# Turning the row picks of a mixture-of-experts loop round: one-hot columns stand, split rows move

## The chip, the cores and the metric

The kernel runs on one core of one Trainium2 chip. The metric is the device time in microseconds (us) of one execution; before the change the median of three runs is 2247.96 us.

## What is computed

A two-layer transformer block on 256 latent tokens and 256 context tokens of width 1024, all in float32. Each layer has three parallel token mixers (two attentions and a pooling), an output projection, and then a mixture of experts. Context tokens leave the second layer after their keys and values, so the experts see 512 tokens in layer 0 and 256 in layer 1. The part that the change touches:

```python
def hierarchical_moe(h, w_rg, b_rg, w_re, b_re, w_gate, w_up, w_down):
    lg = jnp.dot(h, w_rg, ...) + b_rg                 # 4 groups, the best one is taken
    ...
    top_p, top_i = lax.top_k(jax.nn.softmax(le_g, axis=-1), TOP_K)   # 2 of its 8 experts
    ...
    return expert_dispatch(h, experts, weights, w_gate, w_up, w_down)

def run_block(args):                                  # one of 32 experts, D 1024, hidden 512
    xb, e = args
    return (jax.nn.silu(xb @ w_gate[e]) * (xb @ w_up[e])) @ w_down[e]
```

Every token goes to two experts; an expert holds the rows that fall to it, in the order of the tokens. The results come back weighted and are added to the stream.

## The kernel before

Each engine has its own instruction stream, written out by hand, and engines wait for each other at semaphores. A layer's mixer part comes first (its matrix products use fp32r, a one-pass form, on weights and activations split into a high and a low part, lines 459 to 461). Then the norm, the router and the routing follow, then the loop over the experts, and at last a gather of the saved rows.

**Routing.** VectorE works out in a long chain of small operations (L1339 to L1376) which tokens go to which expert and in which slot; `place1` holds for each token and expert the slot number plus one, or zero. Beside it TensorE turns the normed activations back to rows (L678) and ScalarE copies them into `hr` (L999), tokens on the partitions.

**The loop** (L732 on TensorE, 16 turns of two experts, slots s = 0 and 1 of the weight buffers). An expert's rows are picked by a product with a one-hot matrix: VectorE compares `place1` with slot numbers 1 to 64 (`set_pick`, L1380) and gets for each tile of 128 tokens a matrix of 128 x 64; TensorE multiplies, in float32, with the rows standing and the 64 one-hot columns moving (`pick_x`, L702), 8 chunks of 128 features by 4 token tiles (2 in layer 1). The result is already transposed, features on the partitions, 64 slots wide, and is copied by VectorE (L1437) to `xg`. Then `gate_up` (L711) multiplies the standing 64 slots with the moving weights of gate and up, in two column halves of the array at once. ScalarE applies silu (L1032), VectorE multiplies (L1417), TensorE transposes the hidden rows (`turn_h`, L717), VectorE copies them (L1435), and `down` (L723) multiplies with the down weights. ScalarE copies the result (L1055) and saves it with DMAs on its own queue (L1012): 32 rows, and 32 more if the expert holds over 32.

The order on TensorE for one expert is: gate-up of e, first half of the pick for e + 1, turn of e's hidden rows, second half of the pick, down of e. So each half of a pick stands where TensorE would otherwise wait for silu and for the copy.

**Overflow.** An expert with more than 64 rows is done in further blocks of 64 (an `If` around a `Fori` over all possible blocks, on TensorE, VectorE and ScalarE alike), between gate-up and the turn: pick, copy, gate-up, silu, multiply, turn, copy, down, save.

**Weights.** SyncE's queue loads them, 4 MB for gate and up in four DMAs (L392) and 2 MB for down in two (L396), two experts ahead: the gate-up weights of e + 2 are issued once the hidden rows of e are turned, its down weights once e's down is done, in this order on one queue.

Of the kernel before, what the change touches and what calls it, by code (L numbers as in the profile page):

```python
# [18 lines left out]
F32 = mybir.dt.float32  # L19
F32R = mybir.dt.float32r  # L20
# [3 lines left out]
ALU = mybir.AluOpType  # L24
ACT = mybir.ActivationFunctionType
AX = mybir.AxisListType.X

P = 128
# [25 lines left out]
HALF = BLK // 2  # L54
LATENT, CONTEXT = slice(0, SEQ), slice(SEQ, NTOK)
# [75 lines left out]
def hybrid_block(nc, t, out, counts=None):  # L131
# [4 lines left out]
    with ctx:  # L136
# [48 lines left out]
        def part(base, kib, size, *dims, dt=F32):  # L185
# [18 lines left out]
        xg = [part(arena, 24 + 2 * i, 2, KC, BLK) for i in range(3)]  # L204
        pick = [part(arena, 30 + i, 1, 4, BLK) for i in range(3)]
        hid = [part(arena, 34 + i, 1) for i in range(3)]
        hid_t = [part(arena, 37 + i, 1, 2, P) for i in range(3)]
# [4 lines left out]
        r = part(arena, 16, 8)  # L212
        place1 = part(arena, 33, 1)[:, 0:4 * (NE + 2)].rearrange("p (t e) -> p t e", t=4)
# [39 lines left out]
            hrow_copied r_exp r_onehot r_pos r_exp_done routed pick_set picko_set dest_set xt_done xt_copied  # L253
            gu_done silu_done hid_done0 hid_done1 hidt_done hidt_copied down_done0 down_done1 y_copied0
            y_copied1 xto_done xto_copied guo_done siluo_done hido_done hidto_done hidto_copied downo_done
# [182 lines left out]
        def _(pe):  # L438
# [89 lines left out]
            for l in range(DEPTH):  # L528
# [144 lines left out]
                for tile in range(nt):  # L673
                    for half in range(2):
                        bank = 2 + (2 * tile + half) % 4
                        claim(bank)
                        for c in range(4):
                            mm = pe.transpose(ps[:, bank, c * P:(c + 1) * P], ht[:, 4 * half + c, tile * P:(tile + 1) * P], ident[:, :])  # L678
                        mm.then_inc(g["hturn_done"].sem, g["hturn_done"].tick(l, tile, half))
                        free[bank] = (g["hrow_copied"], (l, tile, half))  # L680
# [10 lines left out]
                nb = w_all // BLK  # L691
# [4 lines left out]
                pe.wait_ge(g["hrow_copied"].sem, g["hrow_copied"].at(l, nt - 1, 1))  # L696

                def pick_x(dst_bank, picks, sem, chunks=range(KC)):

                    for c in chunks:  # L700
                        for tile in range(nt):
                            mm = pe.matmul(ps[:, dst_bank, c * BLK:(c + 1) * BLK], hr[:, tile, c * P:(c + 1) * P], picks[:, tile, :],  # L702
                                           start=(tile == 0), stop=(tile == nt - 1))
                    if chunks[-1] == KC - 1:
                        mm.then_inc(sem, 1)

                def gate_up(bank, xs, w, sem):

                    for k in range(KC):
                        for j in range(2):  # L710
                            mm = pe.matmul(ps[BLK * j:BLK * j + BLK, bank, :].rearrange("p (g n) -> p g n", g=2), xs[:, k, :],  # L711
                                           w[:, k, 512 * j:512 * j + 512].rearrange("p (g n) -> p g n", g=2), start=(k == 0), stop=(k == KC - 1))
                    mm.then_inc(sem, 1)

                def turn_h(bank, src, sem):
                    for c in range(2):
                        mm = pe.transpose(ps[:, bank, c * P:(c + 1) * P], src[:, c * P:(c + 1) * P], ident[:, :])  # L717
                    mm.then_inc(sem, 1)
# [7 lines left out]

                if l == 0:
                    n_more = pe.alloc_register("pe_more")
                    pe.reg_mov(n_more, 0)
                pe.wait_ge(g["pick_set"].sem, (NE + 2) * l + 1)  # L730
                pick_x(0, pick[0], g["xt_done"].sem)
                with pe.Fori(0, NE // 2) as i:  # L732
                    for s in range(2):
                        e, done = 2 * i + s, NE * l + 2 * i + s
                        mine = 16 * l + i
                        pe.wait_ge(g["xt_copied"].sem, done + l + 1)
# [8 lines left out]
                        with pe.If(n > BLK):  # L745
                            with pe.Fori(1, nb) as b:
                                with pe.If(n > b * BLK):
                                    more = pe.snap(n_more, min_val=0, max_val=64)
                                    pe.wait_ge(g["picko_set"].sem, more + 1)
                                    pick_x(7, pick[2], g["xto_done"].sem)  # L750
                                    pe.wait_ge(g["xto_copied"].sem, more + 1)
                                    pe.wait_ge(g["yo_copied"].sem, more + 1)
                                    gate_up(6, xg[2], wgu[s], g["guo_done"].sem)
                                    pe.wait_ge(g["hido_done"].sem, more + 1)
                                    turn_h(7, hid[2], g["hidto_done"].sem)
                                    pe.wait_ge(g["hidto_copied"].sem, more + 1)
                                    down(6, hid_t[2], wd[s], g["downo_done"].sem)
# [47 lines left out]
        def _(act):  # L805
# [68 lines left out]
            for l in range(DEPTH):  # L874
# [121 lines left out]
                for tile in range(nt):  # L996
                    for half in range(2):
                        act.wait_ge(g["hturn_done"].sem, g["hturn_done"].at(l, tile, half))
                        nc.scalar.activation(hr[:, tile, 512 * half:512 * half + 512], ps[:, 2 + (2 * tile + half) % 4, :], ACT.Copy) \  # L999
                            .then_inc(g["hrow_copied"].sem, g["hrow_copied"].tick(l, tile, half))  # L1000
# [6 lines left out]
                nb = w_all // BLK  # L1007

                def save_rows(src, row, signal, first=0, rows=BLK):
                    for j in range(2):  # L1010
                        at = BLK * j + first
                        act.dma_start(y_rows[bass.ds(row, rows), j * 512:(j + 1) * 512], src[at:at + rows, :]) \  # L1012
                            .then_inc(signal.sem, 16)

                if l == 0:
# [6 lines left out]
                    act.sem_inc(g["yo_saved"].sem, 32)  # L1022
# [3 lines left out]
                with act.Fori(0, NE // 2) as i:  # L1026
                    for s in range(2):
# [11 lines left out]
                        with act.If(n > BLK):  # L1039
                            with act.Fori(1, nb) as b:  # L1040
                                with act.If(n > b * BLK):
                                    more = act.snap(n_more, min_val=0, max_val=64)
                                    act.wait_ge(g["guo_done"].sem, more + 1)
                                    nc.scalar.activation(act_g[2], ps[:, 6, 0:256], ACT.Silu).then_inc(g["siluo_done"].sem, 1)
                                    act.wait_ge(g["downo_done"].sem, more + 1)
                                    act.wait_ge(g["yo_saved"].sem, more * 32 + 32)
                                    nc.scalar.activation(ysb[2], ps[:, 6, :], ACT.Copy).then_inc(g["yo_copied"].sem, 1)
                                    act.wait_ge(g["yo_copied"].sem, more + 2)
                                    save_rows(ysb[2], act.snap(row + b * BLK, min_val=0, max_val=2 * NTOK), g["yo_saved"])
# [594 lines left out]
```

## Time and profile before

| | |
|---|---|
| median of 3 runs | 2247.96 us (2247.88 to 2249.99) |
| profiled execution | 2246.29 us, its span in the profile 2244.5 us |
| granted TensorE clock, mean | 0.961 |
| TensorE busy | 2070.9 us, 92% of the span |
| VectorE, ScalarE, GpSimd busy | 647.1, 513.0, 156.2 us |
| read from memory | 537.15 MB |
| expert loop of layer 0, first gate-up to last down | 662.15 to 1285.04 us |
| expert loop of layer 1 | 1690.37 to 2206.21 us |

The slices of the page divide the span into 40 parts of 56.1 us. A float32 matmul stands in the profile as two records, as does its weight load; an fp32r matmul as one. Mean durations of pipelined matmuls overlap, so what one costs in a stream is its group's busy time divided by its count, or the distance in the chain.

### The profile page before, as it was taken

The numbers are of one execution on the slowest core, as the hardware profiler recorded it, in microseconds if no ns is written. First come the engines' busy times: TensorE is split into PE (matmuls) and PEld (weight loads), VectorE is DVE, ScalarE is ACT, GpSimd is POOL, SyncE is SP. The second block draws the span as 40 slices with busy tenths as digits, with TensorE's granted clock in tenths as the row PEclk, the third lists the DMA queues.
The fourth block names the chain that finished last, engine by engine and source line by source line (L and its number), as shares of the span: only waits on it lengthen the run. The fifth ranks groups of instructions, "written<-read, shape, count | busy, mean of one in ns | idle before, by whom it ended". The sixth has DMA issues, their size and how long they took to land.

```text
span 2244.5 us, 31445 instructions
## 1 busy us (share of the span) xinstructions
PE 2070.9 (92%) x11703; PEld 1323.6 (59%) x11704; DVE 647.1 (29%) x1392; ACT 513.0 (23%) x1028; POOL 156.2 (7%) x190
## 2 busy tenths in 40 slices
PE   5899999999979999999999959988979999999995
PEld 2666665678746655556555548766965444454443
DVE  1565354345441010110101056455451101110112
ACT  2444333432230001000000044444130001111111
POOL 0053030000000000000000013231000000000000
PEclk9899999999979999999999979989999999999997
DMA  6445554223158898857688523232457879999993
GB/s 233 167 150 190 204 204 154 102 75 99 47 225 345 357 366 364 366 220 303 265 366 361 224 92 123 75 92 93 151 215 310 335 309 421 421 421 421 421 420 113
DMA packets 95915, 551.01 MB, mean 245 GB/s; under 512 B 14034, under 2 KB 15010, under 8 KB 42596
## 3 DMA queue, kind: packets, MB, share of 16 engines
q1 hardware_dynamic: 83108, 526.89, 59.5%
q0 software_dynamic: 4224, 11.35, 1.8%
q10 hardware_dynamic: 8512, 11.81, 1.5%
q8 instruction: 47, 0.77, 0.1%
q14 instruction: 24, 0.20, 0.0%
HBM read 537.15 MB, written 12.85 MB: 245 GB/s over the span
## 4 chain that ended last, share of the span: by engine, by line
PE 78%; DMA 8%; DVE 6%; ACT 5%; issue 2%; SPq 1%; ACTq 0%; POOL 0%; DVEq 0%; POOLq 0%
PE ps L711 19%; PE ps L702 15%; PE ps L723 9%; PE ps L459 7%; PE ps L461 7%; PE ps L460 7%; DMA moe<-in_w_exp_gate_up_dram 6%; PE ps L577 3%; PE ps L606 2%; PE ps L650 2%; PE ps L588 1%; PE ps L499 1%; ACT w_hi L858 1%; DVE w_lo L1134 1%; DMA arena<-y_rows,dest 1%
## 5 line engine op out<-in xcount | busy, mean ns | idle before, releaser
L711 PE MATMUL ps<-moe,arena 128*64 128x512 f32 x2176 | 484.7, 598 | 10.4 <-DMA moe<-in_w_exp_gate_up_dram 5.4
L702 PEld LDWEIGHTS ps<-arena 128*128 128x128 f32 x3360 | 396.7, 196 | 58.3 <-issue 54.2
L702 PE MATMUL ps<-arena 128*128 128x64 f32 x3360 | 408.1, 280 | 6.0 <-DVE arena L1385 4.4
L711 PEld LDWEIGHTS ps<-moe,arena 128*64 128x64 f32 x2176 | 158.7, 138 | 323.9 <-issue 310.2
L459 PE MATMUL ps<-ht_hi,w_hi 128*128 128x512 f32 (+1 forms) x736 | 269.2, 366 | 20.9 <-DVE ht_lo L1157 18.2
L460 PE MATMUL ps<-ht_lo,w_hi 128*128 128x512 f32 (+1 forms) x736 | 258.0, 351 | 0.0
L461 PE MATMUL ps<-ht_hi,w_lo 128*128 128x512 f32 (+1 forms) x736 | 257.7, 350 | 0.0
L723 PE MATMUL ps<-moe,arena 128*64 128x512 f32 x1088 | 250.1, 602 | 2.1 <-DVE arena L1429 2.1
L1417 DVE TENSOR_TENSOR arena<-aux,ps 128x256 f32<-128x256 f32 x64 | 27.0, 421 | 687.5 <-ACT aux L1032 687.5
L1134 DVE TENSOR_TENSOR w_lo<-ws,w_hi 128x1024 fp32r<-128x1024 f32 (+1 forms) x124 | 151.0, 1220 | 246.7 <-ACT w_hi L858 246.6
L459 PEld LDWEIGHTS ps<-ht_hi,w_hi 128*128 128x128 f32 x736 | 140.2, 190 | 72.1 <-issue 43.4
L858 ACT ACTIVATE w_hi<-ws 128x1024 fp32r<-128x1024 f32 (+1 forms) x124 | 127.4, 1027 | 198.8 <-PE ps L461 160.7
L1055 ACT ACTIVATE arena<-ps 128x512 f32<-128x512 f32 x64 | 38.2, 597 | 533.2 <-PE ps L723 533.2
L461 PEld LDWEIGHTS ps<-ht_hi,w_lo 128*128 128x128 f32 x736 | 140.3, 191 | 18.6
L460 PEld LDWEIGHTS ps<-ht_lo,w_hi 128*128 128x128 f32 x736 | 140.6, 191 | 15.8
L723 PEld LDWEIGHTS ps<-moe,arena 128*64 128x64 f32 x1088 | 72.4, 137 | 125.1 <-issue 117.8
L1547 POOL DMA_INDIRECT arena<-y_rows,dest x12 | 12.5, 1040 | 1633.5 <-ACTq L1067 946.7
L1032 ACT ACT_TABLE_LOAD x32 | 41.1, 1283 | 241.4 <-PE ps L711 241.4
L577 PE MATMUL ps<-arena 64*128 64x512 f32 (+1 forms) x192 | 87.2, 576 | 0.0
L1437 DVE COPY arena<-ps 128x512 f32<-128x512 f32 x64 | 44.3, 692 | 142.5 <-PE ps L702 142.5
L1032 ACT ACTIVATE aux<-ps 128x256 f32<-128x256 f32 x64 | 24.5, 383 | 201.0 <-PE ps L711 200.6
L1435 DVE COPY arena<-ps 128x256 f32<-128x256 f32 x64 | 27.2, 425 | 119.4 <-PE ps L717 119.4
(207 smaller groups left out, 1844.3 us busy)
## 6 DMA issues: line engine op xcount, KB each, us to landing
moe<-in_w_exp_gate_up_dram SPq DMA_DIRECT2D x256, 1024.0 KB, 10.7
moe<-in_w_exp_down_dram SPq DMA_DIRECT2D x128, 1024.0 KB, 11.8
moe<-in_w_mod_dram SPq DMA_DIRECT2D x32, 1536.0 KB, 6.9
ws<-in_w_in_dram SPq DMA_DIRECT2D x92, 512.0 KB, 4.0
y_rows<-arena ACTq DMA_DIRECT2D x164, 64.0 KB, 5.7
ws<-in_w_branch_dram SPq DMA_DIRECT2D x16, 512.0 KB, 3.5
ws<-in_w_out_dram SPq DMA_DIRECT2D x16, 512.0 KB, 3.4
aux<-in_rpb_a_dram POOLq DMA_DIRECT2D x64, 64.0 KB, 2.6
```

The lines of the kernel that those rows point to most:

```text
L459: pe.matmul(ps[:, bank, 0:cols], w[:, k, :], a_hi, start=(i == 0), stop=False)
L460: pe.matmul(ps[:, bank, 0:cols], w[:, k, :], a_lo, start=False, stop=False)
L461: mm = pe.matmul(ps[:, bank, 0:cols], w_lo[:, slot, k, :], a_hi, start=False, stop=(k == rows[-1]))
L577: mm = pe.matmul(score_bank[:, qt, 0:n], q_of(kind)[rows, h // 2, q0 + qt * P:q0 + (qt + 1) * P], kt_of(kind, h)[:, keys], start=True, sto ...
L606: mm = pe.matmul(pv_bank[HD * hh:HD * hh + HD, 0:SEQ], v_of(kind, 2 * pair + hh, tile + (4 - n)), prob_t[hh][:, tile, :], start=(tile == 0 ...
L650: mm = pe.matmul(ps[:, 2 + 3 * (n % 2) + b, 0:w_all], w[:, (4 * b + k) % 8, :], ys[b][:, k, 0:w_all], start=(k == 0), stop=(k == 3))
L702: mm = pe.matmul(ps[:, dst_bank, c * BLK:(c + 1) * BLK], hr[:, tile, c * P:(c + 1) * P], picks[:, tile, :], start=(tile == 0), stop=(tile ...
L711: mm = pe.matmul(ps[BLK * j:BLK * j + BLK, bank, :].rearrange("p (g n) -> p g n", g=2), xs[:, k, :], w[:, k, 512 * j:512 * j + 512].rearra ...
L723: mm = pe.matmul(ps[BLK * j:BLK * j + BLK, bank, :], src[:, k % 2, BLK * (k // 2):BLK * (k // 2) + BLK], w[:, k, 512 * j:512 * j + 512], s ...
L858: nc.scalar.activation(w_hi[:, i % 2, 0:m], ws[:, slot, 0:m, :], ACT.Copy) \
L1032: nc.scalar.activation(act_g[s], ps[:, 2 + s, 0:256], ACT.Silu).then_inc(g["silu_done"].sem, 1)
L1134: v.tensor_tensor(w_lo[:, ws_slots[item], 0:m], ws[:, ws_slots[item], 0:m, :], w_hi[:, i % 2, 0:m].bitcast(F32), ALU.subtract).then_inc(g[ ...
```

## The change

Rows and one-hot columns change places in the pick. `hr` is kept as two fp32r arrays, `hr_hi` (ScalarE's copy, rounded) and `hr_lo` (VectorE subtracts, before the routing is finished). The one-hot matrix is built for two experts at once, 128 x 128, and stands; the rows move, 512 features at a time, high and low part into the same sum. The result has slots on the partitions, so it is copied (`xs`) and turned by eight transposes (`turn_x`), then copied again (`xg`). This is done once per pair: the pick behind the gate-up of slot 0, in two halves around the turn of the hidden rows, the transposes behind the gate-up of slot 1 in the same way. Both stand after the overflow blocks now, and after the wait for the down weights. An overflow block holds 32 slots instead of 64, and its three products run in four column quarters of the array, of 256 columns each. Some buffers move: the routing's scratch goes to `aux`, for which ScalarE waits once before the loop; GpSimd loses two waits ahead of the gather.

```diff
+MORE = 32
-                for tile in range(nt):
-                    for half in range(2):
-                        bank = 2 + (2 * tile + half) % 4
...
-                        free[bank] = (g["hrow_copied"], (l, tile, half))
+                for n in range(2 * nt):
+                    bank = n % 6
...
+                    free[bank] = (g["hr_lo_set"], (l, n))
...
-                def pick_x(dst_bank, picks, sem, chunks=range(KC)):
-
-                    for c in chunks:
-                        for tile in range(nt):
-                            mm = pe.matmul(ps[:, dst_bank, c * BLK:(c + 1) * BLK], hr[:, tile, c * P:(c + 1) * P], picks[:, tile, :],
-                                           start=(tile == 0), stop=(tile == nt - 1))
+                def pick_x(half):
+
+                    for tile in range(nt):
+                        for rows in (hr_hi, hr_lo):
+                            mm = pe.matmul(ps[:, 7 * half, :], pick[:, tile, :], rows[:, tile, 512 * half:512 * half + 512],
+                                           start=(tile == 0 and rows is hr_hi), stop=(tile == nt - 1 and rows is hr_lo))
+                    if half:
+                        mm.then_inc(g["xs_done"].sem, 1)
+
+                def turn_x(half):
+                    for c in range(4):
+                        at = (4 * half + c) * P
+                        mm = pe.transpose(ps[:, 7 * half, c * P:(c + 1) * P], xs[:, at:at + P], ident[:, :])
+                    if half:
+                        mm.then_inc(g["xt_done"].sem, 1)
...
+                def more_slots(more, wgu_e, wd_e):
+
+                    pe.wait_ge(g["picko_set"].sem, more + 1)
+                    for tile in range(nt):
+                        for rows in (hr_hi, hr_lo):
+                            for j in range(4):
+                                mm = pe.matmul(ps[quarters[j], 1, 0:256], pick_o[:, tile, :], rows[:, tile, 256 * j:256 * j + 256].bitcast(F32),
+                                               start=(tile == 0 and rows is hr_hi), stop=(tile == nt - 1 and rows is hr_lo))
+                    mm.then_inc(g["xso_done"].sem, 1)
+                    pe.wait_ge(g["xso_copied"].sem, more + 1)
+                    for c in range(2):
+                        mm = pe.transpose(ps[:, 1, c * P:(c + 1) * P], xs_o[:, c * P:(c + 1) * P], ident[:, :])
...
+                    for k in range(KC):
+                        at = P * (k % 2) + MORE * (k // 2)
+                        for j in range(4):
+                            w = wgu_e[:, k, 512 * (j // 2):512 * (j // 2) + 512].rearrange("p (g n) -> p g n", g=2)
+                            mm = pe.matmul(ps[quarters[j], 6, 0:256].rearrange("p (g n) -> p g n", g=2), xg_o[:, at:at + MORE],
+                                           w[:, :, P * (j % 2):P * (j % 2) + P], start=(k == 0), stop=(k == KC - 1))
...
-                        gate_up(2 + s, xg[s], wgu[s], g["gu_done"].sem)
-
-                        pe.wait_ge(g["pick_set"].sem, done + 2 * l + 2)
-                        pick_x(0, pick[1 - s], g["xt_done"].sem, range(4))
+                        gate_up(2 + s, s, wgu[s])
                         n = pe.value_load(n_of[0:1, bass.ds(e, 1)], min_val=0, max_val=NTOK)
                         pe.wait_ge(wd_in[s].sem, (mine + 1) * 32)
                         pe.nop(nofuse=True)
                         with pe.If(n > BLK):
-                            with pe.Fori(1, nb) as b:
-                                with pe.If(n > b * BLK):
...
+                            with pe.Fori(BLK // MORE, w_all // MORE) as b:
+                                with pe.If(n > b * MORE):
+                                    more_slots(pe.snap(n_more, min_val=0, max_val=64), wgu[s], wd[s])
...
+                        if s == 0:
+                            pe.wait_ge(g["pick_set"].sem, pick0 + i + 2)
+                        else:
+                            pe.wait_ge(g["xs_copied"].sem, pair0 + i + 2)
+                        next_pair = turn_x if s else pick_x
+                        next_pair(0)
                         pe.wait_ge(hid_done[s].sem, mine + 2)
-                        turn_h(1, hid[s], g["hidt_done"].sem)
-                        pick_x(0, pick[1 - s], g["xt_done"].sem, range(4, KC))
+                        turn_h(hid[s])
+                        next_pair(1)
...
+                act.wait_ge(g["dest_set"].sem, g["dest_set"].at(l, 2))
...
                 chain(v.memset(place1[:, :, :], 0.0))
+                for n in range(2 * nt):
+                    dve.wait_ge(g["hr_hi_set"].sem, g["hr_hi_set"].at(l, n))
+                    cols = slice(512 * (n % 2), 512 * (n % 2) + 512)
+                    v.tensor_tensor(hr_lo[:, n // 2, cols], ps[:, n % 6, :], hr_hi[:, n // 2, cols].bitcast(F32), ALU.subtract) \
+                        .then_inc(g["hr_lo_set"].sem, g["hr_lo_set"].tick(l, n))
...
+                def set_pair(e):
+
+                    out = pick[:, 0:nt, :].rearrange("p t (j n) -> p t j n", j=2)
+                    v.tensor_tensor(out, place1[:, 0:nt, bass.ds(e, 2)].unsqueeze(3).broadcast_to([P, nt, 2, BLK]),
+                                    slots1[:, 0:BLK].unsqueeze(1).unsqueeze(1).broadcast_to([P, nt, 2, BLK]), ALU.is_equal) \
+                        .then_inc(g["pick_set"].sem, 1)
...
+                def copy_xs():
+                    v.tensor_copy(xs[:, 0:512], ps[:, 0, :])
+                    v.tensor_copy(xs[:, 512:1024], ps[:, 7, :]).then_inc(g["xs_copied"].sem, 1)
+
+                def copy_xg():
+                    v.tensor_copy(xg[:, 0:4, :], ps[:, 0, :].rearrange("p (k n) -> p k n", n=P))
+                    v.tensor_copy(xg[:, 4:8, :], ps[:, 7, :].rearrange("p (k n) -> p k n", n=P)).then_inc(g["xt_copied"].sem, 1)
...
-                pool.wait_ge(g["pick_set"].sem, (NE + 2) * (l + 1))
-                pool.wait_ge(g["xt_copied"].sem, (NE + 1) * (l + 1))
```

## Rows read from the trace of the kernel before

**Rows 1.** The page's slices: gigabytes per second in each of the 40.

```profile
GB/s 233 167 150 190 204 204 154 102 75 99 47 225 345 357 366 364 366 220 303 265 366 361 224 92 123 75 92 93 151 215 310 335 309 421 421 421 421 421 420 113
```

**Rows 2.** Windows: busy us (instructions) per engine, then granted clock, DMA share, GB/s.

```profile
655.00:664.00 9.00, 8.13 (x36) 6.72 (x37) 0.69 (x1) 0.00 (x0) 0.00 (x0) 0.50 0.00 0
1066.00:1122.00 56.00, 53.16 (x310) 30.34 (x308) 6.03 (x13) 4.22 (x7) 0.00 (x0) 0.94 0.68 264
1851.00:1964.00 113.00, 111.53 (x640) 56.43 (x638) 13.88 (x32) 12.72 (x20) 0.00 (x0) 1.00 1.01 421
1989.00:2202.00 213.00, 204.98 (x1148) 102.48 (x1147) 24.30 (x56) 22.71 (x35) 0.00 (x0) 1.00 0.98 408
```

**Rows 3.** Groups by form: busy us, mean ns of one, idle before and releasers.

```profile
L702 PE MATMUL ps<-arena 128*128 128x64 f32 x3360 | 408.1, 280 | 6.0 <-DVE arena L1385 4.4 <-DVE arena L1380 1.4
L702 PEld LDWEIGHTS ps<-arena 128*128 128x128 f32 x3360 | 396.7, 196 | 58.3 <-issue 54.2 <-DVE arena L1385 2.3 <-DVE arena L1380 1.8
...
L499 PE MATMUL ps<-moe,cond 128*32 128x384 f32 x512 | 50.7, 515 | 8.3 <-DMA moe<-in_w_mod_dram 5.9 <-DVE modv L1117 2.3
...
L1437 DVE COPY arena<-ps 128x512 f32<-128x512 f32 x64 | 44.3, 692 | 142.5 <-PE ps L702 142.5
...
L1134 DVE TENSOR_TENSOR w_lo<-ws,w_hi 128x512 fp32r<-128x512 f32 x8 | 5.5, 692 | 7.1 <-ACT w_hi L858 7.1
```

**Rows 4.** Chain of waits, layer 0: start us, us, what (longest pieces).

```profile
647.37 13.93 PE ps L702 x64
662.15 9.07 PE ps L711 x32
...
674.94 0.23 PE ps L717 x2
...
700.18 6.87 PE ps L711 x32
...
718.09 6.87 PE ps L711 x32
```

**Rows 5.** Timeline, layer 1, behind a gate-up that ends at 1882.54.

```profile
1882.81 1.28 ACT L1032 ACT_TABLE_LOAD   x1 [6.33 <-PE ps L711]
1884.11 0.38 ACT L1032 ACTIVATE aux<-ps 128x256 f32<-128x256 f32 x1
...
1885.00 0.44 PE L717 MATMUL ps<-ident,arena 128*128 128x128 f32 x2 [0.37 <-DVE arena L1417]
```

**Rows 6.** Chain of waits, output projection of layer 0, 512 columns, fp32r.

```profile
619.62 0.23 PE ps L459
```

**Rows 7.** Chain of waits, layer 1.

```profile
1682.38 7.08 PE ps L702 x32
...
1701.35 0.44 PE ps L717 x2
...
1731.68 3.80 PE ps L702 x32
...
1821.99 3.80 PE ps L702 x32
...
2008.39 7.09 PE ps L711 x32
...
2191.63 7.09 PE ps L711 x32
2202.60 3.61 PE ps L723 x16
```

**Rows 8.** Timeline, layer 0, around the two overflow blocks.

```profile
975.64 10.93 PE L702 MATMUL ps<-arena 128*128 128x64 f32 x96
...
1001.27 0.43 PE L717 MATMUL ps<-ident,arena 128*128 128x128 f32 x2 [1.27 <-issue]
...
1009.71 1.87 ACTq L1012 DMA_DIRECT2D y_rows<-arena  x4
...
1051.43 10.96 PE L702 MATMUL ps<-arena 128*128 128x64 f32 x96
```

More of the change, by code:

```diff
@@ L54 @@
 HALF = BLK // 2
+MORE = 32
+AHEAD = 4
+PAIRS = NE // 2
 LATENT, CONTEXT = slice(0, SEQ), slice(SEQ, NTOK)
@@ L203, in hybrid_block @@
         hr = part(arena, 0, 16, 4, D)
[L204 to L207, printed above, removed]
+        hr_hi, hr_lo = (placed(n, [P, 4, D], ARENA_AT + kib * 1024, F32R) for n, kib in (("hr_hi", 0), ("hr_lo", 16)))
+        ht_flat = ht[:, :, :].rearrange("p a b -> p (a b)")
+        xg, xs = part(ht_flat, 0, 4, KC, P), part(ht_flat, 4, 4)
+        xs_o, xg_o, pick_o = part(ht_flat, 8, 1), part(ht_flat, 9, 1), part(ht_flat, 12, 0.5, 4, MORE)
+        pick = placed("pick", [P, 4, 2 * BLK], HT_AT + 10 * 1024, F32R)
+        hid = [part(arena, 34 + i, 1) for i in range(2)]
+        hid_o, hid_t_o = part(arena, 36, 0.5), part(arena, 36.5, 0.5)
+        hid_t = [part(arena, 37 + i, 1, 2, P) for i in range(2)]
         ysb = [part(arena, 40 + 2 * i, 2) for i in range(3)]
@@ L725, in down @@
                     mm.then_inc(sem, 1)
+                quarters = [slice(MORE * j, MORE * j + MORE) for j in range(4)]
+                def more_slots(more, wgu_e, wd_e):
[9 more added lines that the diff above has]
+                        mm = pe.transpose(ps[:, 1, c * P:(c + 1) * P], xs_o[:, c * P:(c + 1) * P], ident[:, :])
+                    mm.then_inc(g["xto_done"].sem, 1)
+                    pe.wait_ge(g["xto_copied"].sem, more + 1)
+                    pe.wait_ge(g["yo_copied"].sem, more + 1)
+                    for k in range(KC):
[4 more added lines that the diff above has]
+                                           w[:, :, P * (j % 2):P * (j % 2) + P], start=(k == 0), stop=(k == KC - 1))
+                    mm.then_inc(g["guo_done"].sem, 1)
+                    pe.wait_ge(g["hido_done"].sem, more + 1)
+                    pe.transpose(ps[:, 1, 0:P], hid_o[:, :], ident[:, :]).then_inc(g["hidto_done"].sem, 1)
+                    pe.wait_ge(g["hidto_copied"].sem, more + 1)
+                    for k in range(4):
+                        for j in range(4):
+                            mm = pe.matmul(ps[quarters[j], 6, 0:256], hid_t_o[:, quarters[k]], wd_e[:, k, 256 * j:256 * j + 256],
+                                           start=(k == 0), stop=(k == 3))
+                    mm.then_inc(g["downo_done"].sem, 1)
                 if l == 0:
@@ L995, in _ @@
                     .then_inc(g["logits_copied"].sem, g["logits_copied"].tick(l))
[L996 to L1000, printed above, removed]
+                for n in range(2 * nt):
+                    act.wait_ge(g["hturn_done"].sem, g["hturn_done"].at(l, n))
+                    nc.scalar.activation(hr_hi[:, n // 2, 512 * (n % 2):512 * (n % 2) + 512], ps[:, n % 6, :], ACT.Copy) \
+                        .then_inc(g["hr_hi_set"].sem, g["hr_hi_set"].tick(l, n))
                 for step in range(2):
@@ L1013, in save_rows, with save_more @@
                             .then_inc(signal.sem, 16)
+                act.wait_ge(g["dest_set"].sem, g["dest_set"].at(l, 2))
+                def save_more(row):
+                    for j in range(4):
+                        act.dma_start(y_rows[bass.ds(row, MORE), 256 * j:256 * j + 256], ysb[2][MORE * j:MORE * j + MORE, 0:256]) \
+                            .then_inc(g["yo_saved"].sem, 16)
                 if l == 0:
@@ L1473, in _ @@
                 w_all = width(l)
-                nt, nb = w_all // P, w_all // BLK
+                nt = w_all // P
                 if l:
```

121 lines of the change are left out of this document (60 added, 61 removed).

## The prediction

> **What bounds the kernel now.** I read the page's slices first [rows 1]. The two stretches at 345 to 367 GB/s and at 421 GB/s are the expert loops of layer 0 (slices 12 to 21) and layer 1 (30 to 39). The reader is to see that the same loop, with the same 6.29 MB of weights per expert, moves them faster in layer 1. The chain of waits says why: in layer 0 two experts' gate-up groups start 17.91 us apart, 718.09 - 700.18, with nothing but TensorE between them [rows 4]. That is gate-up 6.87, down 3.58 [rows 4, 7], the transposes of the hidden rows 0.23 and 7.2 us of row picks at L702. Layer 0 is TensorE's. In layer 1 the picks are half as many. At first the loop runs ahead of what the queues deliver; from about 1989 on it waits for gate-up weights every pair: six pairs take 2191.63 - 2008.39 = 183.24 us [rows 7], 30.54 us a pair or 15.27 an expert, with the DMA share at 1.01 and 421 GB/s [rows 2]. Layer 1 ends on the transfers, and 15.27 us is the floor that layer 0 would meet too.
>
> **The picks.** The form view gives a pick's matmul two records of 408.1 / 3360 = 0.121 us each, and its weight load 396.7 / 3360 = 0.118 us [rows 3]: 64 columns move while 128 are loaded, so the load sets the pace. Before, a pair in layer 0 has 64 such matmuls, 15.5 us. After, 128 one-hot columns stand, 512 row columns move, and a pair has 2 halves x 4 tiles x 2 parts = 16 matmuls of one fp32r record. Steady fp32r matmuls of that form take 0.227 us each, loads hidden (0.23 in the chain) [rows 6]: 3.6 us. New are eight transposes, at 0.23 / 2 = 0.115 each [rows 4] 0.9 us. In layer 1, 32 matmuls (7.7 us) become 8 (1.8) and the same 0.9.
>
> **New stalls inside a pair.** Before, half a pick covered the way from gate-up to the transposed hidden rows. With the table load (once per pair, slot 0) that way is 2.46 us: 1.28 + 0.38 + the multiply, from the gate-up's end at 1882.5 to 1885.00 [rows 5]; without it 1.2. After, slot 0 has half a pick behind gate-up (1.8 in layer 0, 0.9 in layer 1), slot 1 four transposes (0.46). Stalls: 0.64 + 0.74 in layer 0, 1.55 + 0.74 in layer 1, and 0.25 for the second copy of slot 1. So TensorE's pair is 2 gate-ups, 2 downs, 2 turns, pick, transposes and stalls: 13.74 + 7.16 + 0.46 + 3.6 + 0.9 + 1.6 = 27.5 us in layer 0 (35.8 before), and 26.7 in layer 1 (29.3 before, with 7.7 of picks and one uncovered 0.2). Both lie below 30.54: both loops go over to the transfers, with 3 us of slack a pair. VectorE's pair copies (four of 0.69 [rows 3]) and the wider one-hot lie under down and gate-up (3.58 and 6.87) and cost nothing; without that cover they'd cost some 3.4 us a pair, and that too would first use up the slack. The weights wait now stands ahead of the next pick on TensorE; down weights land 5.1 us behind gate-up weights, inside a gate-up of 6.87. GpSimd's two dropped waits had long been met when the last rows are saved: nothing.
>
> **Before the loop.** The low parts are 8 subtractions (4 in layer 1) in VectorE's routing chain, which sets the end there; priced by the same shape elsewhere at 0.69 [rows 3]: +5.5 and +2.8 us. Only ScalarE's copies lay there before, beside it. The new prologue runs at a granted clock of 0.50, as the old one [rows 2], so TensorE work costs double. Layer 0: one-hot 0.7 (from 646.9 + 5.5 = 652.4), picks 16 x 0.45 = 7.3, copies 1.5, transposes 1.85, copies 1.5, gate-up can start at 665.4 (662.15 before [rows 4]). Layer 1: picks from 1682.38 + 2.9 [rows 7], 3.6 + 1.5 + 1.85 + 1.5, start at 1693.8 (1690.37 before). The first gate-up took 9.07 and 8.70 as the clock came back on the way; with pauses in front I take 11.4, bounds 9 and 13.7. With 2.7 to the transposes, the first slot comes free at 679.5 in layer 0 (675.2 before [rows 4]) and at 1707.9 in layer 1 (1701.8 [rows 7]).
>
> **The overflow blocks.** Two experts in each layer hold more than 64 rows (17 and 20; 2 and 7 by their place in the chain) [rows 7, 8], each with one block, so each holds 65 to 128. The view can't say whether more than 96: that would be a second block of 32. I take none. A block of 32 has 64 records of 256 columns, four side by side, for the pick (32 in layer 1), 64 for gate-up, 32 for down. The nearest row is the modulation product, four side by side at 384 columns, 50.7 / 512 = 0.099 a record [rows 3]; scaled by columns 0.06. Between 0.06 and 0.09: 12.7 to 17.4 us with a copy, two transposes and their hops more than before. Then the loops: before, six empty turns in layer 0 left TensorE idle 1.27 us after down, with no releaser but issue [rows 8], and two in layer 1 none, so an empty turn is some 0.5 to 0.8 us. Now thirteen and five follow: 6 to 9 and 1 to 3 us uncovered. All in all a block delays its slot by 23 us in layer 0 (bounds 18 to 28) and 16.5 in layer 1 (13 to 20); before, 1001.27 - 975.64 less the half pick of 3.7 is 21.9, and with half the pick 18.4.
>
> **The sum.** DMA start 0.8 us after the slot is free, landing 1.5 after. Layer 1 before, as a test: 1701.8 + 0.8 + 30 x 15.27 - 5.09 + 1.5 = 2157.1 for the last gate-up weights without idle queues; they came at 2191.5, so 34 us idle. Worked out: expert 2's slot frees 29.3 + 18.4 = 47.7 us after the first one's, the queues hold 30.5 + 0.8: 17; expert 7's delay of 19 less what five experts regain (0.64 each): 16; 33 in all.
> Layer 1 after: expert 2 frees its slot 26.7 + 16.6 = 43.3 on, idle 12.7; expert 7's 16.1 less 5 x 1.92 regained, 6.5; 19 in all. 1707.9 + 455.3 + 19.2 = 2182.4, and 12.8 for the last gate-up (7.1), transposes and down: 2195.2 against 2206.2 [rows 7]: -11.
> Layer 0 after: the same with 4.3 us for fourteen half-block saves (128 KB at 421 GB/s; one is in [rows 8]). At expert 17 the queues hold 20.4 us when gate-up starts, and the slot normally frees after 8.3: 11.3 of the 22.4 us delay are absorbed, idle 11. Expert 20 has regained 4.2 of 24: 20. 679.5 + 455.3 + 4.3 + 31 + 12.8 = 1182.9 against 1285.0: -102.
> Together -113: 2246.3 (the profiled execution, span 2244.5) becomes 2133. The median of the runs shown is 1.7 above it: 2135.
>
> A rule speaks against this. The Trainium skill (HBM Reference, Specifications) gives a core about 358 GB/s of its pair's memory. By it 12.85 MB a pair need 35.9 us, no gain in layer 0. The trace doesn't agree where one core runs: 421 GB/s.
>
> **Rivals.**
> (A) As summed: 2135, own range 2115 to 2150. For it the test above; 0.58.
> (B) Second blocks of 32. For: four experts over 64, none provably under 97. Against: few hold even 64. Each adds a block less its gaps, 16 us in layer 0, 13 in layer 1, nothing absorbs it: one or two give 2148 to 2166, all four 2193. 0.24.
> (C) TensorE keeps the end of a pair: the slack of 3 us goes into sequencer work at the register load and branches ahead of the next pick, and into clock dips as after expert 20, whose window has a clock of 0.94 [rows 2], 3.3 of its 56 us. At 32.5 us a pair: 30 x 1.0 in layer 0, some 15 in layer 1: 2165 to 2182. 0.10.
> (D) Slower than before: the pauses of a pair bring the clock to half for much of it. The gain is gone at 113 / 32 = 3.5 us a pair above 30.54, which is 13 to 15 of the 24 to 26 us of TensorE's work at 1.2 GHz. With half the work at that clock a pair takes 40.5 and 38.7, 290 us more: 2425. Against: with 8 us idle in 213 layer 1's end keeps 1.00 [rows 2]. 0.04. The Trainium skill (TensorE: Matmul & The Clock Gate, A second HAM failure mode) tells of such a loop, which idles briefly between groups and pays for the return again and again.
> (E) The change brings nothing, as layer 0's transfers keep to their 367 GB/s [rows 1], 35 us a pair, and the later start eats the rest: 2244 to 2250. The same instructions give 421 in layer 1; 0.01.
> (F) Cheap blocks and an early clock: 2100 to 2114. 0.03.
>
> **How the numbers follow.** The time is A's, 2135. Below 2114 lie 0.06, above 2182 (D, E, four second blocks, the worse of C) about 0.1. A measurement here can't tell less than 0.2% (4.5 us) from no change. Faster is A, B, C, F: 0.95; same is E: 0.01; slower is D: 0.04.
>
> **What would show it.** In layer 0 gate-up groups 30.5 to 31 us apart per pair, DMA at 421, a DMA wait of 2 to 3 us ahead of slot 0's gate-up; pick records 0.227 us; the first gate-up at 665 and 1694; each overflow block some 23 and 16 us; layer 0's loop ends near 1183, layer 1's loop is 501 us long. Wrong would be the prediction with a pair over 31 us and no DMA wait, more than four blocks, or a clock under 1.00 in steady pairs.

## The result, and the profile after

The changed kernel takes 2141.18 us (median of 4, 2135.30 to 2145.59) beside 2248.97 before (4 runs): a ratio of 0.951, 95% interval 0.948 to 0.955. The forecast was 2135 with a range of 2114 to 2182. The profiled execution took 2137.22 us with a span of 2135.3: 109 us less than before, where the sum said 113.

The page's slices come first: the granted clock in tenths, and below it GB/s:

```profile
PEclk9899999999998999999999799999979999999997
GB/s 225 182 133 213 187 207 168 139 55 99 104 147 240 415 421 421 421 311 300 360 420 421 156 104 94 73 97 107 168 236 257 421 378 421 421 421 421 420 421 109
```

Layer 0's stretch stood at 345 to 367 [rows 1] and stands at 415 to 421 now, but for a hole from the eighteenth slice on, where the blocks are. In layer 1 the slices of 309 to 335 ahead of the long run of 421 have become 257 (with the first block in it), 421 and 378. The windows show a steady stretch of either layer and then both whole loops (length; busy us and instructions of TensorE, its weight loads, VectorE, ScalarE and GpSimd; granted clock, DMA share, GB/s):

```profile
790.00:902.00 112.00, 99.83 (x458) 40.22 (x456) 19.46 (x36) 11.42 (x19) 0.00 (x0) 1.00 1.02 421
1824.00:2070.00 246.00, 216.01 (x935) 77.06 (x937) 36.78 (x72) 25.98 (x40) 0.00 (x0) 0.94 1.01 421
660.00:1184.00 524.00, 461.60 (x2318) 190.79 (x2316) 86.27 (x173) 52.67 (x83) 0.00 (x0) 0.97 0.92 378
1595.00:2097.00 502.00, 440.19 (x2118) 161.96 (x2118) 79.89 (x171) 52.75 (x84) 0.00 (x0) 0.95 0.93 386
```

In the first two the DMA share of 1.02 and 1.01 leaves the 16 DMA engines no idle time, and TensorE is idle for 11 and 12%; the whole loops stand at 378 and 386, so the queues do idle somewhere. The chain of waits in layer 0, in the steady part and at the end of the loop:

```profile
1106.82 18.95 DMA moe<-in_w_exp_gate_up_dram
1125.82 7.11 PE ps L723 x32
1137.36 18.95 DMA moe<-in_w_exp_gate_up_dram
...
1180.69 3.68 PE ps L735 x16
```

and in layer 1:

```profile
1990.07 17.24 DMA moe<-in_w_exp_gate_up_dram
2007.36 8.81 PE ps L723 x32
2020.61 17.24 DMA moe<-in_w_exp_gate_up_dram
...
2093.23 3.68 PE ps L735 x16
```

The transfer now stands in every pair of these two stretches (not in those right behind the blocks, where TensorE is late), and consecutive ones start 30.54 us apart, 1137.36 - 1106.82 and 2020.61 - 1990.07: layer 1's old floor [rows 7], now in layer 0 as well, where the pair had been 35.8 [rows 4]. Gate-up in layer 1 takes 8.81 instead of 7.09, part of it at half clock. Behind a gate-up at full clock TensorE waits 1.02 and then 2.56 us for weights ahead of the two following ones (1808.96 and 1824.14), behind one of 8.81 it waits not at all and then 2.09; the pair stays at 30.54, and nothing is lost.

The picks' groups by form (busy us, mean ns, idle before), which answer to [rows 3]:

```profile
L707 PE MATMUL ps<-hr_hi,pick 128*128 128x512 f32 x204 | 90.1, 442 | 20.6 <-issue 11.6 <-DVE pick L1435 8.9
L707 PE MATMUL ps<-hr_lo,pick 128*128 128x512 f32 x204 | 83.3, 408 | 0.0
...
L1446 DVE COPY ht<-ps 128x512 f32<-128x512 f32 x34 | 23.5, 692 | 38.7 <-PE ps L707 38.7
```

3360 records, two to a matmul, have become 408. A mean of 408 ns overlaps the next record; 8 of them take 1.85 us in the steady loop, 0.231 each.

The prologue of layer 0, chain of waits:

```profile
645.40 3.42 DVE hr_lo L1419 x6
...
649.00 1.27 DVE hr_lo L1419 x2
...
651.99 0.70 DVE pick L1435
...
652.74 5.66 PE ps L707 x16
...
659.76 1.11 PE ps L715 x8
...
662.32 7.11 PE ps L723 x32
```

The first gate-up of layer 0 starts at 662.3, as before (662.15 [rows 4]), and takes 7.11, not 9.07. Layer 1's starts at 1595.34 and takes 8.66.

Last, the timeline of TensorE around the first overflow block of layer 0 (start, us, what, idle before it and what ended that):

```profile
933.09 3.66 PE L760 MATMUL ps<-moe,ht 128*32 128x256 f32 x64 [0.52 <-DVE ht L1497]
...
938.18 1.93 PE L768 MATMUL ps<-moe,arena 128*32 128x256 f32 x32 [0.38 <-DVE arena L1501]
948.77 1.10 PE L715 MATMUL ps<-ident,ht 128*128 128x128 f32 x4 [8.65 <-issue]
...
951.08 4.77 PE L735 MATMUL ps<-moe,arena 128*64 128x512 f32 x16
```

Behind the block TensorE stands still for 8.65 us with no releaser ("issue": it waits for nothing that the profile shows), and what follows runs at half clock at first: 4.77 for a down product that takes 3.65 otherwise. Four experts had a block, one each. Behind the second block of layer 0 the pause is 8.71 us, behind each of layer 1's two it is 2.72.

### The profile page after: what moved, and what is told of

It reads as the page before. It is cut to its first block, busy times and chain, and to the rows that moved or that the text cites. A ratio compares the mean times of both kernels' runs of the same rounds, so it can differ in the third digit from the quotient of the medians.

```text
span 2135.3 us, 27115 instructions
## 1 busy us (share of the span) xinstructions
PE 1852.5 (87%) x9411; PEld 1052.3 (49%) x9412; DVE 695.0 (33%) x1446; ACT 512.3 (24%) x1028; POOL 154.7 (7%) x190
## 4 chain that ended last, share of the span: by engine, by line
PE 60%; DMA 19%; DVE 8%; ACT 6%; issue 4%; ACTq 1%; SPq 1%; POOL 0%; DVEq 0%; POOLq 0%
DMA moe<-in_w_exp_gate_up_dram 17%; PE ps L723 15%; PE ps L466 8%; PE ps L468 7%; PE ps L467 7%; PE ps L735 4%; PE ps L584 3%; PE ps L613 2%; PE ps L657 2%; PE ps L707 2%; PE ps L595 1%; PE ps L506 1%; SPq L399 1%; ACT w_hi L902 1%; PE ps L729 1%
## 5 line engine op out<-in xcount | busy, mean ns | idle before, releaser
L723 PE MATMUL ps<-moe,ht 128*64 128x512 f32 x2048 | 469.9, 613 | 46.5 <-DMA moe<-in_w_exp_gate_up_dram 43.1
L723 PEld LDWEIGHTS ps<-moe,ht 128*64 128x64 f32 x2048 | 152.6, 141 | 357.2 <-issue 299.8
L735 PE MATMUL ps<-moe,arena 128*64 128x512 f32 x1024 | 237.2, 606 | 2.4
L468 PEld LDWEIGHTS ps<-ht_hi,w_lo 128*128 128x128 f32 x736 | 140.7, 191 | 18.6
L735 PEld LDWEIGHTS ps<-moe,arena 128*64 128x64 f32 x1024 | 68.7, 138 | 133.9 <-issue 117.9
L707 PE MATMUL ps<-hr_hi,pick 128*128 128x512 f32 x204 | 90.1, 442 | 20.6 <-issue 11.6
L707 PE MATMUL ps<-hr_lo,pick 128*128 128x512 f32 x204 | 83.3, 408 | 0.0
L707 PEld LDWEIGHTS ps<-hr_hi,pick 128*128 128x128 f32 x204 | 40.4, 198 | 52.9 <-issue 41.8
L969 ACT ACTIVATE moe<-moe,stat 128x256 f32<-128x256 f32 x64 | 32.2, 503 | 123.8 <-DVE stat L1287 66.0
```

What stands on the lines that cost most here:

```text
L468: mm = pe.matmul(ps[:, bank, 0:cols], w_lo[:, slot, k, :], a_hi, start=False, stop=(k == rows[-1]))
L707: mm = pe.matmul(ps[:, 7 * half, :], pick[:, tile, :], rows[:, tile, 512 * half:512 * half + 512], start=(tile == 0 and rows is hr_hi), st ...
L735: mm = pe.matmul(ps[BLK * j:BLK * j + BLK, bank, :], src[:, k % 2, BLK * (k // 2):BLK * (k // 2) + BLK], w[:, k, 512 * j:512 * j + 512], s ...
```

## The experiments

Nine kernels ran. Where two kernels are set side by side below, each one's time was taken beside the kernel before on its own chip.

**1. The two loops with half the bytes.** How much of the pair is TensorE's own work? In the kernel after, the loop's experts (not the first two of a layer) load half of each weight tensor, and the rest of a buffer keeps what the first two left there:

```diff
-                        ks = slice(2 * i, 2 * i + 2)
+                        ks = slice(2 * i, 2 * i + part_of)
```

with `part_of = 1` in the loop. 

> The changed kernel; in the loop each expert DMA loads one of its two row chunks, so half the bytes of experts 2 to 31 (the rest of a slot stays from experts 0 and 1; outputs of those experts are not the reference's). Theory: the loops end on the transfers, and TensorE's own pair is 27.5 us in layer 0 and 26.7 in layer 1: pairs of this length, no DMA wait ahead of gate-up, layer 1's loop 501 us down to about 463 and layer 0's 524 to about 500. Rival: TensorE, with sequencer work and clock dips, has come down only to about 30.5 itself: pairs stay within 0.5 us of 30.5. The clock in layer 1 tells whether the DMA waits are what lowers it (0.94 to 1.00).

The kernel took 2059.36 us. Chain of waits, gate-up pieces one pair apart, in layer 0 and in layer 1:

```profile
690.48 6.89 PE ps L723 x32
...
717.93 2.14 PE ps L723 x9
...
1927.33 6.89 PE ps L723 x32
...
1953.86 6.43 PE ps L723 x29
```

27.45 and 26.53 us a pair with no wait for weights: the forecast's 27.5 and 26.7, measured. The loops took 493 and 457 us, where 500 and 463 had been expected. The granted clock is 1.00 in the steady pairs of both layers, so without the waits for weights layer 1 keeps it. The pauses behind the blocks stayed at 8.65 and 8.71 us. So the kernel after pays 78 us for the transfers' floor (2137.22 - 2059.36), and the pauses are none of their doing.

**2. The kernel before with the same cut.** 

> The kernel before with the same halved loads (outputs not the reference's in the same way). Theory: layer 0 is TensorE's, its pair stays at 35.8 us; layer 1 goes back to TensorE's 29.3 throughout, its loop from 516 to about 508. Rival: transfers share in layer 0's 35.8 (contention or late weights): its pair falls by more than 0.3 us.

2233.37 us in its one execution, 13 less than the 2246.29 of before: 7.5 of them in layer 1's loop, now 508.3 us (508 expected). Two gate-up groups of layer 0, then two of layer 1:

```profile
715.20 6.87 PE ps L711 x32
...
751.03 6.87 PE ps L711 x32
...
2105.18 6.89 PE ps L711 x32
...
2134.43 6.89 PE ps L711 x32
```

35.83 and 29.25 us: before, TensorE alone set layer 0, and layer 1 had 1.3 us a pair on top of it. Together with experiment 1: the change takes 8.4 us a pair from TensorE in layer 0, of which 5.3 reach the time.

**3. The high part alone.** No low part: no subtractions, and half the pick records. 

> The changed kernel without the low part: no subtractions, picks with the high part alone (8 and 4 matmuls a pair), so the rows are only as exact as the high part. Theory: inside the loops the picks lie in TensorE's slack, so only what stands before the loops counts: 8 and 4 subtractions of 0.65 to 0.69 and half of the first pick (2.8 and 1.8 us): 12 to 14 us less, 2124 to 2128. Rival: the picks are still on the path in the loops, 1.8 and 0.9 us a pair: 40 to 55 us less, 2085 to 2100.

```diff
-                for n in range(2 * nt):
-                    ...
-                    v.tensor_tensor(hr_lo[:, n // 2, cols], ps[:, n % 6, :], ...)
-                        for rows in (hr_hi, hr_lo):
+                        for rows in (hr_hi,):
```

2116.72 us (2115.81 to 2126.18, 4 runs), ratio 0.943 (0.939 to 0.946). The steady pairs stayed at the floor:

```profile
1112.31 8.81 PE ps L723 x32
1142.84 8.81 PE ps L723 x32
```

So 1.8 us of picks a pair less are worth nothing inside the loop, which excludes the rival. The span is 21 us shorter all the same, more than the 12 to 14 expected, and where it lies can be read: layer 0's first gate-up starts at 656.37, 5.9 us sooner (it starts at 662.3 to 667.1 in the seven kernels that share the code up to there); with the two blocks of layer 0, whose picks are halved too, its last one comes 13.0 sooner; the rest, 8.5 of the 21.5 us by which layer 1's first comes sooner, lies between the loops and wasn't taken apart. From layer 0's last gate-up to layer 1's first, the same seven take 417.7 to 423.9 us in their profiles (this one 415.1), so up to 6 us there is scatter. The low part costs ahead of the loops and in the blocks, not in the steady pairs.

**4. Doubled picks.** Each pick's 8 matmuls of a half issue twice, into the same sums. 

> The changed kernel with every pick done twice, the second writing the same sums again: 3.6 us a pair more in layer 0, 1.8 in layer 1, 5.7 and 3.6 ahead of the loops. Theory: slack of 3.0 and 3.9 us a pair takes nearly all of it; layer 0's pair goes to 31.1 at most, layer 1's stays 30.54: 2150 to 2162. Rival: picks are still on the path of every pair: 85 us and more, over 2220.

```diff
-                    for tile in range(nt):
+                    for tile in [*range(nt), *range(nt)]:
```

2166.24 us in its one execution, above the 2150 to 2162 expected. The chain in layer 0 has no transfer left:

```profile
719.59 6.46 PE ps L723 x30
...
731.57 6.87 PE ps L723 x32
738.44 3.90 PE ps L707 x16
...
749.81 6.89 PE ps L723 x32
```

Seven pairs of the timeline's gate-up groups, 718.99 to 933.48, are 30.64 us apart each, with no wait for weights. The slack of a pair in layer 0 is 3 us (30.54 - 27.45), as forecast: 3.6 us more of picks, of which some fall into TensorE's short stalls (27.45 and 3.6 would be 31.05), lengthen the pair by 0.1. What the kernel loses, 29 us, it loses in layer 0: 7.8 at the start and 21.6 in the loop (531.0 us from the first gate-up to the last, 509.4 before the doubling), where no slack is left to make up for a delay: the kernel after runs pairs of 27.45 us behind its blocks (1026.33 to 1053.80 and on to 1081.24), this one 30.6. Layer 1, whose picks are half as many, loses nothing: 489.0 us in either kernel.

**5. The overflow loop cut in two.** What is the pause of 8.65 us? The theory was TensorE's walk through thirteen turns without a block. In this kernel the turns up to 128 slots stand in one loop and the rest in a second one behind a branch, on three engines (below, TensorE's, shortened). 

> The changed kernel, with the overflow loop cut in two on TensorE, VectorE and ScalarE: blocks up to slot 128, and the rest only inside a test for more than 128 rows. After a block one empty turn is left instead of thirteen (layer 0) and five (layer 1). Theory: the idle time of TensorE behind a block (8.65, 8.71, 2.72, 2.72 us in the changed kernel, released by nothing but issue) is the sequencer running through empty turns; it falls to under 1.5 us each, some 18 us of delay go, and as the transfers are dry at that point nearly all of it comes off the time: 2118 to 2124 where the changed kernel has 2137 to 2141. Rival: the idle time is the return from the branch (instruction fetch), whatever the number of turns: then it stays and so does the time.

```diff
-with pe.Fori(BLK // MORE, w_all // MORE) as b:
+with pe.Fori(BLK // MORE, P // MORE) as b:
     with pe.If(n > b * MORE):
         more_slots(...)
+with pe.If(n > P):
+    with pe.Fori(P // MORE, w_all // MORE) as b:
+        with pe.If(n > b * MORE):
+            more_slots(...)
```

2148.31 us (2142.57 to 2152.71, 5 runs), ratio 0.955 (0.952 to 0.957): no gain, where 2118 to 2124 had been expected. The pauses behind the blocks were gone, and others had come, one or two in most pairs of layer 0. Pauses over 1 us in 680 to 770, chain of waits:

```profile
686.96 2.71 issue
...
723.94 3.87 issue
...
765.30 2.58 issue
```

The page's line on the instruction queue, packets, MB and share:

```profile
q8 instruction: 97, 1.59, 0.3%
```

The kernel after has 47 packets with 0.77 MB there, and one pause (at 684.45, of 2.59 us) in its first pairs. TensorE lost 48 us to such pauses in layer 0 (17 of them), where the kernel after lost 20 (3). The loop's text had grown by a second copy of the block's code for each slot, which never runs, and twice the packets of instructions were fetched. The pauses stand in pairs without a block too, where the new code is only jumped over. The Trainium skill (Runtime: NRT & Kernel Launch, Instruction fetch mechanics) says the like: a taken branch to a page outside the window forces a fetch before execution goes on. The packets and the pauses agree with it; the fetch behind a single pause no view here shows. Half of the theory held, and the test had spoiled its own result.

**6. The loop ends at the expert's own count.** No empty turns, and no second copy (below, TensorE's edit, shortened). 

> The changed kernel with the overflow loop bounded by the expert's own row count (first slot 64, step 32, end n), on TensorE, VectorE and ScalarE: no empty turn and no second copy of the block's code. Theory: the cut loop (e1) took the idle time behind a block away but made the loop body too long to stay in the instruction buffer (instruction queue 47 to 97 packets, stalls of 2.5 to 3.9 us in layer 0's turns); this one keeps the body short: 47 packets, no such stalls, under 1.5 us behind a block, 2118 to 2126. Rival: the stalls come from something else that the loop's new branches bring: then they show here too and the time stays over 2135.

```diff
-with pe.Fori(BLK // MORE, w_all // MORE) as b:
-    with pe.If(n > b * MORE):
-        more_slots(...)
-        pe.reg_add(n_more, n_more, 1)
-    pe.nop(nofuse=True)
+with pe.Fori(BLK, n, MORE) as b:
+    more_slots(...)
+    pe.reg_add(n_more, n_more, 1)
```

and so on ScalarE and VectorE. 2108.38 us (2102.51 to 2110.67, 5 runs), ratio 0.936 (0.934 to 0.938): 1.6% below the kernel after, the fastest of all. The instruction queue has 47 packets again, and behind the block TensorE goes straight on:

```profile
942.15 1.93 PE L768 MATMUL ps<-moe,arena 128*32 128x256 f32 x32 [0.39 <-DVE arena L1498]
944.02 0.66 PE L715 MATMUL ps<-ident,ht 128*128 128x128 f32 x4
...
945.41 3.65 PE L735 MATMUL ps<-moe,arena 128*64 128x512 f32 x16
948.90 7.04 PE L723 MATMUL ps<-moe,ht 128*64 128x512 f32 x32
```

The way from a blocked expert's gate-up to the next one is 26.0, 33.0, 26.4 and 24.2 us, where it was 36.9, 43.2, 33.0 and 28.8: 10.9, 10.2, 6.6 and 4.6 us less. That is more than the 8.7 and 2.7 us of the pauses (the half clock behind them, and turns that lay under the block's last products), hence the gain beyond the 2118 to 2126 expected. It goes through to the end: layer 0's loop is 18 us shorter, layer 1's 10, the span 28.7. Per turn, 13 and 5 of them, some 0.8 and 1.1 us. What in a turn costs isn't shown: an empty one compares, counts, and also jumps over the block's code.

**7. TensorE's loop alone.** The same edit on TensorE only; the other two keep their turns. 

> Only TensorE's overflow loop ends at the expert's own count; ScalarE and VectorE keep their 14 and 6 turns. Theory (the pause behind a block is TensorE's own walk through its empty turns): the two pauses of 8.7 us in layer 0 and the two of 2.7 us in layer 1 vanish as they did when all three engines were cut, nothing waits for ScalarE or VectorE instead for more than 2 us a block, and the time is 2104 to 2116 us. Rival (the other engines' empty turns are as late, and merely lay under TensorE's): behind a block TensorE waits 5 us or more for VectorE's multiply or for the next copy, and the time is 2125 to 2140.

2119.40 us (2117.86 to 2128.05, 4 runs), ratio 0.943 (0.938 to 0.947), span 2116.7: between the two theories' times. Timeline behind the first block:

```profile
943.50 0.60 PE L715 MATMUL ps<-ident,ht 128*128 128x128 f32 x4
948.37 5.35 PE L735 MATMUL ps<-moe,arena 128*64 128x512 f32 x16 [4.27 <-DVE arena L1504]
```

TensorE's own turns are worth 18.6 us of the 28.7 (by the two loops alone, 18.4 of 28.1). With them gone VectorE's are next: the copy of the hidden rows at L1504 comes 4.27 us late behind one block and 1.37 behind the other of layer 0, and in experiment 6, without VectorE's turns, it isn't late. Neither theory alone holds; the turns count on each engine that the next expert needs.

**8. A copy that never runs.** Is it really the length of the loop's text? Experiment 6, and on TensorE a second copy of the block behind a condition that no expert meets (below, shortened, against experiment 6). 

> The kernel of e5 with a second copy of the block's code on TensorE behind a test that is never true (more than 511 rows), so only the length of the loop body changes. Theory: the length is what costs: about 100 instruction packets, stalls of 2.5 to 4 us two or three times a pair in layer 0, 20 to 30 us slower than e5. Rival: code that isn't run costs nothing: within 4 us of e5.

```diff
 with pe.Fori(BLK, n, MORE) as b:
     more_slots(...)
     pe.reg_add(n_more, n_more, 1)
+    with pe.If(n > NTOK - 1):
+        more_slots(...)
```

2124.40 us (2108.06 to 2130.01, 4 runs), ratio 0.942 (0.938 to 0.946), 16 above experiment 6 where 20 to 30 were expected. The intervals only just part, and one of the four executions, 2108.06, is as fast as experiment 6; the profiled one took 2122.52, and its span is 14 us longer. The pauses of 700 to 800 in the chain of waits:

```profile
722.87 4.37 issue
...
763.19 2.64 issue
...
780.45 2.77 issue
```

The page's instruction queue:

```profile
q8 instruction: 69, 1.13, 0.2%
```

The same work and 22 packets more (about 100 had been expected), with pauses of 20 us in layer 0 against 2.6. In layer 1, whose picks have half the tiles, there is but one of 2.7. The pauses at 722.87 to 780.45 stand ahead of any block, where the new test isn't reached: the length of what is jumped over is what differs there. Part of them falls into the slack: layer 0's loop is 7.5 us longer than in experiment 6 and layer 1's 4.2; the remaining 2.4 lie outside the loops, within the scatter there. So the pauses are shown, and what they cost in the median is less certain. At what length the fetching sets in wasn't measured.

**9. Blocks of 64 in the changed kernel.** That part undone: 64 slots, two side by side with 512 columns, six empty turns in layer 0 and two in layer 1. 

> The changed kernel with overflow blocks of 64 slots as before (two column halves of 512, picks from both parts), all else as changed. Theory: block for block 32 slots gain little: the three products take 6.9 + 7.1 + 3.65 instead of 3.7 + 3.7 + 1.9 us in layer 0, 8 us more, but 6 empty turns follow instead of 13, 7 us less; in layer 1 3.4 + 7.1 + 3.65, 5 to 6 more, and 2.7 less: 4 to 10 us slower in all than the changed kernel, 2142 to 2150. Rival: the smaller block pays by its products alone, 25 us or more slower.

2146.94 us (2143.31 to 2150.30, 4 runs), ratio 0.953 (0.951 to 0.956); its interval overlaps that of the kernel after, so in the time as a whole no difference is shown. Timeline behind the first block:

```profile
941.33 7.09 PE L759 MATMUL ps<-moe,ht 128*64 128x512 f32 x32 [0.78 <-DVE ht L1498]
...
950.31 3.65 PE L769 MATMUL ps<-moe,arena 128*64 128x512 f32 x16 [0.52 <-DVE arena L1502]
955.20 0.65 PE L715 MATMUL ps<-ident,ht 128*128 128x128 f32 x4 [1.23 <-issue]
```

From the first pick to the end of down the block takes 22.0 us (932.00 to 953.96) instead of 12.2 (927.93 to 940.11), and the pause 1.23 instead of 8.65. In layer 0, first to last gate-up are 509.5 us apart against 509.4: what the block of 32 saved in products it gave back in turns. In layer 1, where only five empty turns follow, the block of 32 is ahead by 10.6, twice what was expected: 489.0 against 499.6.

## Why the prediction came out right

**The floor.** 30.54 us a pair in both layers, at 421 GB/s and a share of 1.01 to 1.02: as written, and the largest term. The rule that the prediction sets against it (the Trainium skill, HBM Reference, Specifications) is none for this case: the section gives the 358 GB/s as a core's share while both cores of a pair stream, and says that a core alone measures well above it, as the 421 here does. Rival E, a layer 0 that keeps its 35 us a pair, is refuted: that had been TensorE's pace, which half the bytes left at 35.83 (experiment 2).

**TensorE's pair.** 27.5 and 26.7 forecast, 27.45 and 26.53 measured in experiment 1; picks at 0.231 us for the 0.227 assumed. The price of the old picks was a little off, 15.5 us a pair by the whole kernel's mean of 0.121 a record, where the steady loop's 7.2 us an expert make 14.4; it enters no term of the sum. That the slack of 3 us takes picks up came out in experiments 3 and 4. Rivals C and D are refuted for the steady pairs. The clock did fall, to 0.94 in layer 1's steady window, and the forecast had named a clock under 1.00 as a sign against it. That was too strict: a gate-up longer by 1.7 us lies inside the slack of 3.9.

**The stretch before the loops** was mis-sized, in both directions. The eight subtractions took 4.9 us, not 5.5. The clock came back during the first picks (granted clock 0.68 from 652 to 659 and 1.00 from 659 on, where the forecast took the 0.50 of [rows 2]), so these took 5.66, not 7.3, the transposes 1.11, not 1.85, and the gate-up 7.11, not 11.4, below its lower bound of 9. The hidden rows were being turned at 671.71, so the first slot came free some 7 us sooner than 679.5. In layer 1 the clock stayed at 0.50 up to the gate-up: 3.77, 1.98 and 8.66, the last again below the bound. Layer 0's loop ended at 1184.4 all the same, for a forecast of 1183. That is luck: the first slot came free 7 us sooner than forecast, the loop from there on was 9 us longer, and the two misses cancelled. Of the 9 the blocks, below, were 6.5; the rest wasn't taken apart, and the pause of 2.59 us at 684.45, which no term of the sum had, is a candidate.

**The blocks.** One each: rival B, second blocks, is refuted. Records took 0.058 us, just below the bounds of 0.06 to 0.09. The delay of a slot, over the 12.42 or 15.04 us (14.11 for the latter in layer 1) that the way takes without a block, was 24.4 and 28.2 us in layer 0 (23 forecast, bounds 18 to 28, so the second just past them) and 18.9 and 16.3 in layer 1 (16.5, bounds 13 to 20). The uncovered pause was 8.65 and 2.72, in the upper part of the 6 to 9 and 1 to 3; the half clock behind it had not been counted.

**The whole.** Layer 0's end moved by -100.6 us (-102 forecast). Layer 1's loop, first gate-up to the end of down, took 501.6 us (501.4). Between the end of the one and the start of the other lie 410.9 us, where the forecast had 408.8 (1693.8 - 1285.0). The 4 us by which the sum missed the profiled execution are these three, 1.5, 0.2 and 2.1, and 0.1 behind the loops; the 2.1 is less than kernels with the same code differ by there (6 us). The mechanism was right; that the number is this close owes something to the two misses that cancelled. The median is 4 us above the profiled execution, inside its own scatter.

The forecast did not see that the block of 32 was no gain in layer 0, and that 29 us lay in the turns: it had priced them, at 0.5 to 0.8 us, as a cost of the change, without weighing the one against the other. At 0.8 and 1.1 us, half clock behind them included, they were also dearer.

## What to carry to other kernels

Before work is taken from the engine that bounds a loop, measure the next floor from another stage of the same trace: the gain ends at that floor, here 5.3 of the 8.4 us a pair, and with half the bytes both can be seen. A loop over a rare case is paid in its empty turns, on every engine that the following step needs, so a smaller block pays in full only if the loop ends at the count: here it gained nothing over 13 empty turns and 10.6 us over five. Code that never runs can still cost when it lengthens the body of a hot loop; the instruction queue's packets in the profile, and pauses that nothing releases, tell.

## What had not been expected of the hardware

An empty turn of the block loop cost 0.8 us or more of the loop's time, two thirds of it TensorE's own. One copy of a block's code (163 records of matmuls and transposes for each slot in layer 0) that is never executed, on TensorE alone, took the instruction queue from 47 to 69 packets and brought pauses of 2.6 to 4.7 us, at a cost of 12 us in the two loops of the profiled execution; copies on three engines made it 97 packets, and nothing of the turns' 29 us was won. And the granted clock fell in the steady pairs of layer 1 (0.94) but not in those of layer 0 (1.00), with TensorE busy 88% and 89% of the time. The waits for weights have a part in it: with half the bytes and none of these waits it is 1.00 in both layers. But they don't bring it down wherever they stand: with doubled picks layer 1's steady pairs keep 1.00 with a wait of 2.55 us ahead of slot 0's gate-up and 0.1 ahead of slot 1's, and without the low part its last pairs keep it with 2.57 and 1.36. Which pattern of pauses brings it down is open.
